# All 48 window-cache copies from GpSimd's queue inside the latent prompt attention, with the bias work and the row stores inside attention stages

## The reference, cut to what matters

```python
SWA_GROUPS = ((128, 1), (512, 4), (2048, 16))
...
def dilated_group_attend(q_pos, q, kv_all, row0_pos, win, dil, bias):
    nk = win // dil + 1
    dist = jnp.arange(nk, dtype=jnp.int32) * dil
    key_pos = q_pos[:, None] - dist[None, :]
    kv = jnp.take(kv_all, key_pos - row0_pos, axis=1)
    s = jnp.einsum('bqhd,bqjhd->bhqj', q, kv[:, :, :, 0]).astype(jnp.float32) * SWA_SCALE
    s = s + bias.astype(jnp.float32).T[None, :, None, :]
...
        kv_g = jnp.concatenate([prefix, kv_new], axis=1)
        new_bufs.append(kv_g[:, -win:])
        bias = rel_bias[t5_bucket(jnp.arange(win // dil + 1, dtype=jnp.int32) * dil),
                        g * SWA_HEADS_PER_GROUP:(g + 1) * SWA_HEADS_PER_GROUP]
```

## Time and profile before

| what | value |
|---|---|
| median of 3 runs | 3973.1 us (3959.29 to 3975.86) |
| the profiled execution | 3970.43 us |
| its span in the trace | 3968.6 us |
| PE, DVE, ACT, POOL busy | 76%, 41%, 13%, 14% of the span |
| PE's mean granted clock | 0.866 of full speed |

### The profile page before, as it was taken

One profiled execution on the slowest core, in us unless ns is written; L12 is line 12 of the kernel. 1 busy time (PEld: TensorE's weight loads), 2 busy tenths in 40 slices (PEclk: granted clock), 3 DMA queues, 4 the chain that ended last, 5 costly groups with the idle time before them and its releaser, 6 DMA issues. The chain is left out here.

```text
span 3968.6 us, 45440 instructions
## 1 busy us (share of the span) xinstructions
PE 3013.4 (76%) x17585; PEld 2431.6 (61%) x17585; DVE 1611.5 (41%) x3772; ACT 505.9 (13%) x1146; POOL 554.8 (14%) x586
## 2 busy tenths in 40 slices
PE   6767785267667678999999941959659999999960
PEld 3444333055443447999999941625427999999960
DVE  1212000022110213968457477030222968557468
ACT  2133100034211201110000000000311110000000
POOL 0000000000000000112312364000000101411455
PEclk8578897579887789999999975979789999999985
DMA  2033434249867574867967997424432776977998
GB/s 96 3 96 91 152 126 136 67 133 281 243 226 264 197 269 139 281 221 244 409 217 259 409 392 282 169 81 175 165 122 99 267 235 205 409 246 232 405 396 297
DMA packets 280679, 866.60 MB, mean 218 GB/s; under 512 B 33905, under 2 KB 60562, under 8 KB 278199
## 3 DMA queue, kind: packets, MB, share of 16 engines
q1 hardware_dynamic: 206756, 595.46, 44.6%
q0 software_dynamic: 73728, 268.47, 18.0%
HBM read 845.19 MB, written 109.08 MB: 240 GB/s over the span
## 5 line engine op out<-in xcount | busy, mean ns | idle before, releaser
L1934 PE MATMUL ps<-xT,p1e_uT 128*128 128x192 f32 x2048 | 346.4, 329 | 7.6 <-DMA p1e_uT<-in_peer_uT 7.6
L1934 PE MATMUL ps<-xT,p0e_uT 128*128 128x192 f32 x2048 | 345.2, 328 | 6.7 <-DMA p0e_uT<-in_peer_uT 6.4
L1961 PE MATMUL ps<-p0e_S,p_qT 128*128 128x192 f32 x2048 | 345.6, 327 | 0.0
L1961 PE MATMUL ps<-p1e_S,p_qT 128*128 128x192 f32 x2048 | 345.6, 327 | 0.0
L1934 PEld LDWEIGHTS ps<-xT,p1e_uT 128*128 128x128 f32 x2048 | 336.0, 192 | 9.0 <-DMA p1e_uT<-in_peer_uT 8.2
L1934 PEld LDWEIGHTS ps<-xT,p0e_uT 128*128 128x128 f32 x2048 | 334.4, 191 | 8.5 <-DMA p0e_uT<-in_peer_uT 7.9
L1961 PEld LDWEIGHTS ps<-p1e_S,p_qT 128*128 128x128 f32 x2048 | 332.5, 190 | 0.0
L1961 PEld LDWEIGHTS ps<-p0e_S,p_qT 128*128 128x128 f32 x2048 | 332.5, 190 | 0.0
L1683 POOL DMA_INDIRECT p0e_rows<-in_peer_u,p0e_expert x128 | 133.2, 1040 | 699.7 <-DVE p0e_dots L1776 449.2
L1683 POOL DMA_INDIRECT p1e_rows<-in_peer_u,p1e_expert x128 | 133.9, 1046 | 690.9 <-DVE p1e_dots L1776 452.0
L1954 PEld LDWEIGHTS ps<-h_tok 128*128 128x128 f32 x1536 | 189.5, 192 | 9.3 <-DVE h_tok L1803 4.8
(11 more groups left out here) (446 smaller groups left out, 3949.2 us busy)
## 6 DMA issues: line engine op xcount, KB each, us to landing
p_qT<-in_peer_v SPq DMA_DIRECT2D x256, 512.0 KB
p0e_uT<-in_peer_uT SPq DMA_DIRECT2D x128, 512.0 KB
p1e_uT<-in_peer_uT SPq DMA_DIRECT2D x128, 512.0 KB
out_swa_sample<-in_cache_swa_w SPq DMA_DIRECT2D x32, 2040.0 KB, 26.6
m_cache<-in_cache_mem_kv SPq DMA_DIRECT2D x32, 1024.0 KB, 6.1
ms_pages<-in_cache_mla SPq DMA_DIRECT2D x128, 144.0 KB, 2.7
ss_kcache<-in_cache_swa_w SPq DMA_DIRECT2D x72, 256.0 KB, 11.6
ss_vcache<-in_cache_swa_w SPq DMA_DIRECT2D x72, 256.0 KB
```

Source lines behind the costliest of these rows:

```text
L1934: mm = pe.matmul(k.ps[:, SB[i % len(SB)], 0:TD], ur[:, i % NU, c, :], k.xT[:, c, D0:T], start=(c == 0), stop=(c == KC - 1))
L1961: mm = pe.matmul(k.ps[:, c // 2, c % 2 * TD:(c % 2 + 1) * TD], vr[:, i % NV, c * P:(c + 1) * P], S[:, i % SLOTS, :], start=False, stop=(i ...
```

## The change

1. The 48 cache copies leave SP's queue. POOL issues all of them in a row in the `mlp` stage (`copy_caches`), on a semaphore of their own that only the last block of the program waits for. `lat` has no copies now; later projections have the zero rows left, five per job.
2. The products of the bias by distance move into `mlp` (`BiasByDistance`): before `values(u)` of units 1 to 7 PE makes two chunks and ACT evacuates them, in unit 8 one. SP loads their inputs, stores the result, waits for it and issues the three spreading copies in the same stage.
3. The tables `e_bias_p` and `e_bias_s` are loaded by POOL in the `win` stage (`BiasTables`); SP waits for them in `kturn`.
4. The window rows are stored by SP inside `swp`, the memory keys and values inside `m0p` and `m1p` (`Stores`); their own stages are gone. So is the mask's: it is loaded in `qs`.

```diff
+        self.n_cached = len(pieces)
+        return pieces + zero_rows
...
+    def copy_caches(self, eng):
+        for dst, src in self.copies[:self.n_cached]:
+            eng.dma_start(dst, src).then_inc(self.cache_copied, 16)
+        self.n_copied = self.n_cached
...
-def gemm_stage(k, name, jobs):
+def gemm_stage(k, name, jobs, beside=None, copies=COPIES_PER_JOB):
...
             for u in range(U):
                 if u + 1 < U:
                     scores(u + 1)
+                if beside:
+                    beside.tensor(pe, u)
                 values(u)
...
+class BiasByDistance:
+    def of_unit(self, u):
+        return [n for n in range(len(self.chunks)) if 1 + n // 2 == u]
+    def gpsimd(self, pool):
+        pool.memset(self.rel[:, :], DISALLOWED).then_inc(self.filled, 1)
+        self.k.copy_caches(pool)
+    def sync(self, sp):
+        k, io = self.k, self.k.io
+        sp.dma_start(self.hot[:, :, :], io["bucket_hot"]).then_inc(self.landed, 16)
+        sp.wait_ge(self.filled, 1)
+        sp.dma_start(self.rel[0:N_BUCKETS, :], io["rel_bias"]).then_inc(self.landed, 16)
+        sp.wait_ge(self.taken, len(self.chunks))
+        sp.dma_start(io["bias_by_dist"].rearrange("g h n -> h g n"), self.byd[:, :, :]).then_inc(k.by_dist_stored, 16)
+        sp.wait_ge(k.by_dist_stored, 16)
+        for g in range(3):
+            src = bass.AP(io["bias_by_dist"].tensor, g * SWA_H * N_DIST + REP0, [[N_DIST, SWA_H], [0, P], [1, REP_N]])
+            sp.dma_start(io["bias_rep"][g], src).then_inc(k.bias_spread, 16)
...
+class BiasTables:
+    def gpsimd(self, pool):
+        pool.memset(Bs[:, :], 0.0).then_inc(self.zeroed, 1)
+        pool.wait_ge(k.bias_spread, 48)
...
+                    pool.dma_start(Bp[:, h, qb, g, :], src).then_inc(k.bias_tabled, 16)
...
+class Stores:
+    def sync(self, sp):
+        self.begin(sp)
+        sp.wait_ge(self.sem, self.due)
...
-                window_outputs_stage(k, kv)
...
-                bias_stage(k, e)
...
-                act.wait_ge(k.copied, 16 * len(k.copies))
+                act.wait_ge(k.copied, 16 * (len(k.copies) - k.n_cached))
+                act.wait_ge(k.cache_copied, 16 * k.n_cached)
```

More of the change, by code:

```diff
@@ L299, in _ @@
                 repeat(pe, pairs, product)
+        if beside:
+            @block.gpsimd
+            def _(pool):
+                beside.gpsimd(pool)
         @block.scalar
@@ L412, in _, with attend_prompt @@
                     last.then_inc(turned, 1)
-def attend_prompt(k, name, units, cols, scale, mask_scales, out_n=P):
+def attend_prompt(k, name, units, cols, scale, mask_scales, beside=None):
     nc = k.nc
@@ L430, in attend_prompt, with _ @@
         psf = k.ps[:, :, :].rearrange("p b n -> p (b n)")
+        apart = 512 if cols <= 512 else 1024
+        if beside:
+            @block.sync
+            def _(sp):
+                beside.sync(sp)
+            @block.gpsimd
+            def _(pool):
+                beside.gpsimd(pool)
         def width(u):
@@ L864, in _, with store_windows @@
                 pe.transpose(k.ps[0:ROPE, 1, 256:256 + n], rows[0:n, i, 256:288], k.ident[0:n, 0:n]).then_inc(turned, 1)
[L867 to L892, removed]
+def store_windows(k, kv, sp):
+    io = k.io
+    n = 0
+    sp.dma_start(io["kv_new"], kv[0:64, 2, :]).then_inc(k.window_stored, 16)
+    n += 1
+    for g, (w, _) in enumerate(SWA_GROUPS):
+        for c in range(2):
+            cols = slice((c * 3 + g) * GW, (c * 3 + g + 1) * GW)
+            dst = io[f"swa_prompt{g}"][0, 0, :, c].rearrange("w h d -> w (h d)")
+            for i in range(2):
+                r = w - SEQ + i * P
+                if r >= 0:
+                    sp.dma_start(dst[r:r + P, :], kv[:, i, cols]).then_inc(k.window_stored, 16)
+                    n += 1
+            for b in range(DEC_B):
+                dst_s = io[f"swa_sample{g}"][0, b, w - DEC_S:w, c].rearrange("w h d -> w (h d)")
+                sp.dma_start(dst_s, kv[8 * b:8 * b + 8, 2, cols]).then_inc(k.window_stored, 16)
+                n += 1
+    assert n == N_WINDOW_STORES
 def query_stage(k, e):
@@ L1092, in turn_stage, with __init__, gpsimd, tensor @@
+class Stores:
+    def __init__(self, begin, sem, due):
+        self.begin, self.sem, self.due = begin, sem, due
+    def sync(self, sp):
+        self.begin(sp)
+        sp.wait_ge(self.sem, self.due)
+    def gpsimd(self, pool):
+        pass
+    def tensor(self, pe, u):
+        pass
+    def scalar(self, act, u):
+        pass
+def turn_stage(k, name, jobs, stores=None):
     nc = k.nc
@@ L1095, in turn_stage, with _ @@
         block = ctx.enter_context(k.block())
+        if stores:
+            @block.sync
+            def _(sp):
+                stores(sp)
         @block.tensor
@@ L1129, in even_mixer @@
                 e["latent"] = k.sb(c2, "e_latent", [P, 3, first])
-                gemm_stage(k, "lat", [("tok", k.xT, w_in[:, 0:first], 272, e["latent"])])
+                gemm_stage(k, "lat", [("tok", k.xT, w_in[:, 0:first], 272, e["latent"])], copies=0)
                 latent_stage(k, e)
                 query_stage(k, e)
-            with ExitStack() as c2:
-                mask = k.sb(c2, "e_causal", [P, 2, SEQ])
-                mla_prompt(k, e, mask)
+            mla_prompt(k, e)
             mla_sample(k, e)
@@ L1194, in mla_prompt @@
                           "outs": [e["olatT"][:, c, h, qs] for c in range(2)]})
-    attend_prompt(k, "mlp", units, SEQ, MLA_SCALE, 1.0)
+    with ExitStack() as ctx:
+        attend_prompt(k, "mlp", units, SEQ, MLA_SCALE, 1.0, BiasByDistance(k, ctx))
 def mla_sample(k, e):
@@ L1428, in memory_attention @@
                         "outs": [oT[:, 2 * h + c, qs] for c in range(2)]})
-            attend_prompt(k, n_ + "p", units, N_MEM, MEM_SCALE, 1.0)
+            attend_prompt(k, n_ + "p", units, N_MEM, MEM_SCALE, 1.0, Stores(
+                lambda sp: sp.dma_start(io["mem_kv_prompt"][layer, 0].rearrange("(i p) c h d -> p i (c h d)", p=P),
+                                        mkv[:, :, :]).then_inc(k.mem_kv_stored, 16),
+                k.mem_kv_stored, 16 * (layer + 1)))
         with ExitStack() as c1:
```

168 lines of the change are left out of this document (74 added, 94 removed).

## The result

The changed kernel takes 3984.5 us (median of 12 runs, 3972.0 to 3999.1), the kernel before beside it 3965.7 (12 runs): a ratio of **1.0047, 95% interval 1.003 to 1.0064**. The interval leaves out 1, so the change is slower, by 12 to 25 us; that is near the 0.5% (20 us) that the prediction calls no change, and the forecast was 3980. The profiled execution took 3975.2 us, span 3973.4; it is one of the faster ones, 5 us above the profiled execution before, where the medians differ by 19.

The account below looks back on a forecast made before the run. The prediction saw layer 0's mixer as a chain of stages leaving most DMA capacity unused. From 3970.4 us it took 190 of gains and added 200 of loss from the moved copies: 3980 us, range 3890 to 4015.

Parts of the forecast that it names:

- The sum of the gains, 190: Removed store waits, bias stage and weight waits, mainly around `kturn`, `swp` and `m0in`, were to save 190 us.
- 104 forecast: Between `kturn` and `swp`, moving the bias stage away was to save 104 us of 106.
- 35 forecast: `win` up to `kturn`: 27 us from window-row stores, 11 from a second weight wait, less 3 for table loads.
- the clock: Stages behind `m0in` were to get a slightly higher clock: gain 3 us, between 0 and 8.
- The loss, 200: Copies in `mlp` were to delay the page table, so `mls` begins at 416, not 217: loss 199, summed as 200.
- Strict turns: Engines alternate queues packet by packet whatever the size, so SP's small packets each wait 3.0 us: 3980 us, chance 0.60.
- rival B: Small reads get through beside the copies, by several SP packets per turn or small copy packets: 3919 us, chance 0.27.
- POOL itself is not held: In `mlp`, POOL issues a gather in about 1 us, so its 48 copy issues fit into the stage.
- Its other form: Copies run in 4 KB packets, spreads take 0.25 us each, pages begin near 297: loss 138 us.
- Rival C: Copies drain slower from POOL's queue q0, delaying `mls`: slower, 4030 us and above, chance 0.13.
- the 329: Copy rate in GB/s from which down the slower-drain case decides; copies take 13 us more, the sum passes 3993.
- the assumed 255: The 87.3 MB of copies at 343 GB/s were to take 255 us of all engines.

Follow-up runs that it names:

- run 9: The changed kernel with GpSimd issuing the 48 copies (65 KB packets) at the start of `mls`, not `mlp`: 4028.9 us, ratio 1.0157 to the kernel before.
- run 10: The changed kernel with GpSimd issuing the 48 copies at the start of `mls`, in packets of 8,160 bytes: 3972.4 us, ratio 1.0021 to the kernel before.
- run 4: The changed kernel with the three spreading copies reordered so their packets lie on 16 engines, not 4: 3953.0 us, ratio 0.9966 to the kernel before.
- run 7: The changed kernel with copies cut into 8 KB rows and spreading copies on 16 engines: 3968.0 us, ratio 0.9993 to the kernel before.
- run 8: The changed kernel with the 48 copies issued by ScalarE (ACT) at its first unit in `mlp`, not by GpSimd: 3977.1 us (one run).
- run 3: The changed kernel with the 48 copies on GpSimd's queue cut into rows of about 4 KB: 3997.9 us, ratio 1.0086 to the kernel before.

## Why the prediction was right

- **The sum of the gains, 190: measured about 213.** `kturn` to `swp` lost 108 us of 113 (104 forecast). The `win` stage up to `kturn` lost 39 (35 forecast: 27 + 11, less 3 for the table loads). `m0in` 22.7 (22), the window between `m0p` and `m0out` 13.3 and between `m1p` and `m1out` 10 (13 for both stores), `p0q` 8.6 (7), `cin` 7.8 (6), `swp` with `sws` 5.8. Little elsewhere (2 us) goes the other way. The undersized term is the clock, 3 us. In `m0p` and `m0s` the removed wait is 7 of the 13.3 us, and the rest is faster products: PE comes out of a short wait at a high clock. The first scores of `m0p`, before and now, with the wait ahead of them:

```profile
1268.75 3.75 PE L441 MATMUL ps<-m_kT,m_qT 128*128 128x256 f32 x8 [8.09 <-PEq L168]
```

```profile
1303.21 1.97 PE L470 MATMUL ps<-m_kT,m_qT 128*128 128x256 f32 x8 [1.10 <-PEq L182]
```

  The same 8 products take 1.97 us behind a wait of 1.1 us and 3.75 behind one of 8.1; the granted clock of the 10 us from there is 1.00 now, the 2.4 GHz level throughout, and was 0.54 over the 20 us behind them before, nearly all at 1.2 GHz. Behind those 10 us it is 0.60 now, so the gift is short.
- **The loss, 200: measured 218.** The copies began 3 us later than assumed and moved until 397, not 375. A 65 KB packet took 3.1 us and not 3.0, and a packet of the spreads 0.18 us in the mean from 190 to 370 and not 0.08. These 18 us nearly cancel the 23 on the side of the gains, which is luck: the forecast of 3980 owes its last half per cent to two errors of opposite sign.
- **Strict turns** were right, and runs 9 and 10 show them to one packet in 1188. The Trainium skill's rule ("DMA: Bandwidth & Descriptors", Queues, rings and completion order), that an engine drains a whole packet of one ring before it switches, agrees with them; its typical 9 to 17 descriptors per packet would have let some nine of SP's rows through per turn (rival B), and here each small row was a turn of its own.
- **"POOL itself is not held: it issues a gather in about 1 us, 48 issues fit into `mlp`" was wrong.** The issues did fit, 23.5 us of them. But the barrier's DRAIN on GpSimd waits for what it has issued. The sum did not need this, as SP was held 3 us longer; that too is luck, since the prediction had one of two holds of nearly the same length. A reader who had mended only SP's hold on the prediction's word would have won 31 us of 218 (run 4).
- Rival B as a mechanism (several rows per turn) is refuted by run 9, which was some 105 us above what nine rows per turn would give. Its other form, copies in small packets, would not have given its 3919 either: the DRAIN keeps the same end (run 7).
- **Rival C's sign came.** The copies still moved after 390 us, and at 87.3 MB / 284 us = 307 GB/s, with the spreads among them, they were under the 329 from which the prediction lets C decide. (At 329 the copies take 11 us more, not 13: a slip.) With a loss of 218 the forecast's own gains would have given 3998; the 23 us of gains on top brought it back. It is not C's 251 GB/s, and not a property of q0 in the main: full stretches ran at 317 to 350 GB/s, and a 65 KB packet took 3.0 us on SP's queue (the kernel before), 3.1 on GpSimd's and 3.2 on ACT's (run 8). The end was drawn out because only some engines had work left. DMA queues of 370 to 400 us:

```profile
q0 software_dynamic: 70, 2.55, 20.3%
q1 hardware_dynamic: 469, 0.95, 8.4%
```

  Together that is about 4 of 16 engines, as many as carry the spreads. Yet run 4, with the spreads on all 16, needed 284 us as well; how the slower packets, the spreads and the semaphores' packets share the 29 us over the assumed 255 is not shown.
- Its tests: no page before 370, SP's spreading issues over 100 us, PE idle from 220, `mls` of 206 us, `kturn` and `swp` within 2 us, `m0in` of 105 us (in the same cut as the earlier trace rows): all seen.

## What to carry to other kernels

In this kernel a large DRAM-to-DRAM copy is not background work: each small packet that another queue sends meanwhile waits for one of its packets. Price such a copy as (packets of the awaited transfers per engine) x (time of one copy packet), and place it where nothing small is awaited before it is through, in its own queue or in another; up to that point it was free here but for a few us (16 copies in `mlp`, five behind the weights of `aout`, `m0out` and `cout`). And with this barrier, which drains every engine, a stage in which GpSimd issues a DMA does not end before that DMA does, even if no instruction waits for it.

## What the runs showed of the hardware that I had not expected

- GpSimd's DRAIN at a barrier lasts until its DMAs have landed: 63.4, 164.6 and 268.3 us with 16, 32 and 48 copies, ending 1 to 3 us after the last packet. ACT's does not: 0.41 us with 64 us of copies outstanding.
- GpSimd can be stopped at its issues: after 36 copies in 4 KB rows (run 3), for 222 us, until the last of them was through; with the same bytes in 8 KB or 65 KB rows (runs 7 and 4) never. That the number of rows outstanding decides it is the likely reading, not a tested one.
- Rows of 4,080 and of 8,160 bytes gave the same packets, 8,160 bytes and 0.31 to 0.33 us in the median (0.40 to 0.42 in the mean); rows of 65,280 bytes one packet each, 3.1 us. With the spreads on 16 engines the copies took 286 us in rows of 8,160 bytes (run 7) and 284 in rows of 65,280 (run 4), so small packets cost next to no rate here.
